# VectorE's order within a score step: bank evacuations ahead of page sums, pool differences, normalisation products and sample sums

## The reference

```
h = rms_norm(x);  z = h @ w_in            # one projection, 3624 columns
q, k, v, ga, qi, wi, ki, ub, gb, uc, gc = split(z)
att  = softmax attention of 8 heads over the 132 (sample: 64) keys that relu indexer scores choose
pool = (trailing mean over 2/4/8/16 tokens - token) @ pool_w * pool_scale      # from ub
conv = silu(layer_norm(causal depthwise conv of width 31 (cv * sigmoid(cg))))
x    = x + concat(att * silu(ga), pool * silu(gb), conv * silu(gc)) @ w_out
```

## Time and profile before

| | us |
|---|---|
| median of 3 runs | 739.81 |
| lowest and highest run | 735.61, 743.48 |
| the profiled execution, its own time | 738.43 |
| its span from the first to the last instruction | 737.1 |

### The profile page before, as it was taken

The page is one execution under the profiler, slowest core; times in us unless marked ns, Lnnn a source line. Parts: engine busy times, 40 slices in busy tenths (PEclk is TensorE's granted clock), DMA queues, the critical chain, the costliest instruction groups (busy, mean ns, idle before and its releaser), DMA issues.

```text
span 737.1 us, 14658 instructions
## 1 busy us (share of the span) xinstructions
PE 688.2 (93%) x5314; PEld 576.1 (78%) x5314; DVE 521.5 (71%) x1312; ACT 342.5 (46%) x884; POOL 311.1 (42%) x463
## 2 busy tenths in 40 slices
PE   5999989799889989999999998978989898999998
PEld 5987868588787777768999686757878787777797
DVE  4358989899977876445733998999997795722232
ACT  5747536245946433333245762734484643332202
POOL 1403599963947600111250259997384861000000
PEclk9999999899989999999999999999998998999999
DMA  5460240314223525015016213131423164401302
GB/s 206 141 196 19 69 135 30 116 36 145 59 89 112 201 70 199 0 58 174 22 59 190 58 60 101 75 116 36 145 59 89 58 174 145 172 1 58 103 20 109
DMA packets 54984, 71.97 MB, mean 98 GB/s; under 512 B 12977, under 2 KB 30585, under 8 KB 54881
## 3 DMA queue, kind: packets, MB, share of 16 engines
q1 hardware_dynamic: 54802, 70.96, 30.0%
q10 hardware_dynamic: 111, 0.08, 0.0%
HBM read 64.05 MB, written 7.61 MB: 97 GB/s over the span
## 4 chain that ended last, share of the span: by engine, by line
PE 43%; DVE 21%; POOL 14%; ACT 10%; DMA 5%; issue 4%; SPq 2%; DVEq 0%; POOLq 0%; ACTq 0%
PE R L1347 16%; DVE bias L1791 5%; DVE small L1789 4%; PE R L1331 4%; PE R L1332 3%; PE R L1333 3%; POOL small L907 3%; ACT W_r L986 3%; ACT W L986 3%; PE R L1490 3%; DVE W_r L1695 3%; POOL kz L911 3%; PE A L1519 2%; PE A L1277 2%; POOL kz L909 2%
## 5 line engine op out<-in xcount | busy, mean ns | idle before, releaser
L1331 PE MATMUL R<-x_hi,W_r 128*128 128x268 f32 x448 | 138.6, 309 | 5.9 <-DVE cc L1695 1.8
L865 POOL TENSOR_TENSOR W_r<-W,W_r 128x256 fp32r<-128x256 f32 x128 | 92.1, 751 | 114.7 <-ACT W_r L986 114.0
L1333 PE MATMUL R<-x_hi,W_r 128*128 128x268 f32 x448 | 132.4, 295 | 0.0
L1332 PE MATMUL R<-x_lo,W_r 128*128 128x268 f32 x448 | 132.2, 295 | 0.0
L1347 PE MATMUL R<-yT,W 128*128 128x268 f32 (+2 forms) x768 | 124.2, 318 | 0.0
L1347 PEld LDWEIGHTS R<-yT,W 128*128 128x128 f32 x768 | 106.9, 190 | 15.8 <-issue 7.1
L1306 PE MATMUL R<-W_r,x_hi 128*128 128x512 f32 (+2 forms) x252 | 98.8, 392 | 15.1 <-DVE W_r L1695 11.5
L1331 PEld LDWEIGHTS R<-x_hi,W_r 128*128 128x128 f32 x448 | 88.6, 198 | 22.0 <-issue 10.6
L1307 PE MATMUL R<-W_r,x_hi 128*128 128x512 f32 (+2 forms) x252 | 95.6, 379 | 0.0
L1308 PE MATMUL R<-W_r,x_lo 128*128 128x512 f32 (+2 forms) x252 | 95.2, 378 | 0.0
L1332 PEld LDWEIGHTS R<-x_lo,W_r 128*128 128x128 f32 x448 | 88.9, 198 | 0.0
(11 more groups left out here) (277 smaller groups left out, 1300.4 us busy)
## 6 DMA issues: line engine op xcount, KB each, us to landing
W<-in_w_in SPq DMA_DIRECT2D x52, 512.0 KB, 4.8
KV<-in_cache_k SPq DMA_DIRECT2D x32, 256.0 KB, 2.9
W<-in_w_out SPq DMA_DIRECT2D x8, 1024.0 KB, 7.5
KV<-in_cache_v SPq DMA_DIRECT2D x32, 256.0 KB, 3.4
ubx<-qkv_rows SPq DMA_DIRECT2D x16, 256.0 KB, 3.4
out_new_k_prompt<-kz SPq DMA_DIRECT2D x8, 256.0 KB, 2.0
out_new_v_prompt<-V SPq DMA_DIRECT2D x8, 256.0 KB
out_y_prompt<-W SPq DMA_DIRECT2D x8, 256.0 KB
```

The costliest lines, as they stand in the source:

```text
L865: done = pool.tensor_tensor(w_raw(m, W_r)[part], w_raw(m)[part], w_high(m, W_r)[part].bitcast(F32), ALU.subtract)
L1331: pe.matmul(out, hi[:, cols], x_hi[:, kc, toks], start=(kc == 0), stop=False)
L1332: pe.matmul(out, hi[:, cols], x_lo[:, kc, toks], start=False, stop=False)
L1333: m = pe.matmul(out, lo[:, cols], x_hi[:, kc, toks], start=False, stop=(kc == KC - 1))
```

## The change

Within DVE's score step `take` moves from the end of the step to the place behind the sample tokens' top-k, logits and value work and ahead of the normalisation product `on`; and `pool_differences`, `ln_diag`, `ln_mul`, `swish`, `page_scores`, and the sample tokens' sums (of step 26 those behind "isc", and all of step 27) move behind `on`. The first two instructions of step 26 (the reduction and scaling "isc"), step 6's sample dots, the sample tokens' top-k and softmax, and the product `y_s` at the very end of a step stay in their order to `take`. No instruction is added, removed or altered, and the other four engines' programs are the same.

```diff
                 late(n)
-                if n == SX["pool_diff"]:
-                    pool_differences(0)
-                if n == SX["pool_diff2"]:
-                    pool_differences(1)
-                if n == SX["ln_diag"]:
...
-                if n == SX["ln_mul"]:
...
-                if 0 <= n - SX["swish"] < 3:
...
-                b = n - SX["pages"]
-                if 0 <= b < 8:
-                    page_scores(2 * b)
-                    page_scores(2 * b + 1)
                 if n == SX["index_dots"]:
...
                 if n == SX["index"]:
                     sd(lambda: dve.reduce_sum(isc.rearrange("p (g b) -> p g b", g=2), ds[:, :, :, :], AX.X))
                     sd(lambda: dve.tensor_scalar(isc, isc, 1.0 / 16, None, ALU.mult), "isc")
-
-                    dve.wait_ge(*rows_s.at(32))
...
-                if n == SX["index_turn"]:
...
+                if n < len(PLAN):
+                    for u in PLAN[n]:
+                        if u[0] not in ON_ACT:
+                            take(u)
                 if n >= 11 and (n - 11) % 8 == 0:
                     i = (n - 11) // 8
                     dve.wait_ge(*MV_s.at(i + 1))
                     wait_evac(dve, ("turn", i, 0))
                     tile = qT[:, :, START[i]:START[i] + ROWS[i]]
                     on_s.did(dve.tensor_tensor(tile, A[:, 2, :].rearrange("p (c t) -> p c t", c=4)[:, :, 0:ROWS[i]], tile, ALU.mult))
-                if n < len(PLAN):
-                    for u in PLAN[n]:
-                        if u[0] not in ON_ACT:
-                            take(u)
+                if n == SX["index"]:
+                    dve.wait_ge(*rows_s.at(32))
...
+                if n == SX["index_turn"]:
...
+                if n == SX["pool_diff"]:
+                    pool_differences(0)
+                if n == SX["pool_diff2"]:
+                    pool_differences(1)
+                if n == SX["ln_diag"]:
+                    dve.wait_ge(*lnp_s.at(2))
+                    dve.wait_ge(*pd_s.at(PD_END))
+                    for i in range(NT):
+                        r = LN_ROWS[i]
+                        lnd_s.did(dve.tensor_scalar(ln_dg[0:r, 128 * i:128 * i + r], ident[0:r, 0:r], lnr[0:r, i:i + 1], None, ALU.mult))
+                if n == SX["ln_mul"]:
...
+                if 0 <= n - SX["swish"] < 3:
...
+                b = n - SX["pages"]
+                if 0 <= b < 8:
+                    page_scores(2 * b)
+                    page_scores(2 * b + 1)
                 for at, tile, lo, hi in ((29, 2, 0, HALF), (38, 3, HALF, START[4]), (43, 4, START[4], NTOK)):
```

More of the change, by code:

```diff
@@ L2042, in vector_layer @@
                 late(n)
-                if n == SX["pool_diff"]:
-                    pool_differences(0)
-                if n == SX["pool_diff2"]:
-                    pool_differences(1)
-                if n == SX["ln_diag"]:
[L2048 to L2052, removed]
-                if n == SX["ln_mul"]:
-                    wait_evac(dve, ("lnrow", 0, 1))
-                    ln_s.did(dve.tensor_tensor(cc[:, :, :], cc[:, :, :], lnrow.unsqueeze(1).broadcast_to([128, 2, TOK]), ALU.mult))
-                if 0 <= n - SX["swish"] < 3:
-                    if n == SX["swish"]:
-                        dve.wait_ge(*gate_s.at(GATE_OF["gc", 1, 1] + 1))
-                    swish(n - SX["swish"])
-                b = n - SX["pages"]
-                if 0 <= b < 8:
-                    page_scores(2 * b)
-                    page_scores(2 * b + 1)
                 if n == SX["index_dots"]:
@@ L2124, in vector_layer @@
                     on_s.did(dve.tensor_tensor(tile, A[:, 2, :].rearrange("p (c t) -> p c t", c=4)[:, :, 0:ROWS[i]], tile, ALU.mult))
-                if n < len(PLAN):
-                    for u in PLAN[n]:
-                        if u[0] not in ON_ACT:
-                            take(u)
+                if n == SX["index"]:
+                    dve.wait_ge(*rows_s.at(32))
+                    sd(lambda: dve.tensor_tensor(t8[:, :, 0:ID], zis[:, 0:256].rearrange("p (h d) -> p h d", h=IH),
+                                                 zis[:, 256:288].unsqueeze(1).broadcast_to([8, IH, ID]), ALU.mult))
+                    sd(lambda: dve.reduce_sum(d8, t8[:, :, 0:ID], AX.X))
+                    sd(lambda: stt(e8, d8, 0.0, zis[:, 384:392], ALU.max))
+                    sd(lambda: dve.reduce_sum(sc8[:, 256:257], e8, AX.X))
+                    sd(lambda: dve.tensor_scalar(sc8[:, 256:257], sc8[:, 256:257], 1.0 / 16, None, ALU.mult))
@@ new lines, in vector_layer @@
+                if n == SX["index_turn"]:
+                    sd(lambda: dve.tensor_tensor(t8, rows8[:, 0:512].rearrange("p (h d) -> p h d", h=8),
+                                                 rows8[:, 512:1024].rearrange("p (h d) -> p h d", h=8), ALU.mult))
+                    sd(lambda: dve.reduce_sum(snw, t8, AX.X))
+                    sd(lambda: dve.tensor_tensor(sn.rearrange("p (b h) -> p b h", b=8), E8.rearrange("p (b h) -> p b h", b=8),
+                                                 snw.unsqueeze(1).broadcast_to([8, 8, 8]), ALU.mult))
+                    dve.wait_ge(*sit_s.at(1))
+                    sd(lambda: dve.tensor_copy(sc8[:, 0:256], A[0:8, 3, 0:256]))
@@ new lines, in vector_layer @@
+                if n == SX["ln_mul"]:
+                    wait_evac(dve, ("lnrow", 0, 1))
+                    ln_s.did(dve.tensor_tensor(cc[:, :, :], cc[:, :, :], lnrow.unsqueeze(1).broadcast_to([128, 2, TOK]), ALU.mult))
+                if 0 <= n - SX["swish"] < 3:
+                    if n == SX["swish"]:
+                        dve.wait_ge(*gate_s.at(GATE_OF["gc", 1, 1] + 1))
+                    swish(n - SX["swish"])
+                b = n - SX["pages"]
+                if 0 <= b < 8:
+                    page_scores(2 * b)
+                    page_scores(2 * b + 1)
```

## The result

The changed kernel takes **743.28 us** (median; 738.68 to 749.19) against 738.45 for the kernel before on the same chip: ratio **1.0063** (95%: 1.0041 to 1.0084). It is 0.63% slower, which is 4.65 us of 738.45. The forecast was 738.0, 1.8 us faster than the 739.81 that it started from. The time lies in the forecast's range, and a change within 1% was its likeliest case, but the sign is wrong. Ratios leave out disturbed executions, so they need not equal the quotient of two medians.

A forecast was written before the change was run, and what follows sets the result against it. The prediction took PE, busy 93% of the span, as the bound, so only its idle time could move. +0.4 and -2.2 us summed to -1.8, from 739.81 to 738.0 us, range 733.5 to 744.5.

The forecast's parts named there:

- Step 12: Pool differences and diagonals end 1.6 and 2.2 us later; PE's stop before lnrow0 grows to about 3.5 and 3.4 us.
- Step 16: At `weigh`, ACT's earlier copy gives part of the delay back; PE released +0.5 and +0.3 to +0.8 us late.
- the swap of slow units: Second layer: gc01 turns slow at the low clock, +1.3 us, and gc10 turns fast, -1.3 us.
- the prediction's own sign: The prediction counts as wrong if PE leaves step 16 more than 1 us late.
- the second layer's -2.2 us of steps 26 to 28: ga31 starts 3.2 or 1.5 us earlier, depending on ga30's clock; -2.2 us taken.
- the last page sum: Page sums of steps 18 to 25: the last comes +0.8 us in the first layer, -0.4 in the second.
- +0.4 for steps 26 to 28 of the first layer: PE's ga31 starts 0.4 us later, as ga21's evacuation comes 1.5 us later.
- The move of the sums: Step 26: 1.33 us of sample sums move behind the evacuation; turn2 starts 0.5 and 1.7 us earlier.
- step 28: First layer: 2.75 us of moved work precedes its mask, gate and top-k; ga21's evacuation 1.5 us later.
- The diagonals' rival: Step 12's delay not given back, plus slow gc01: 5.1 us together, 744.8 us; chance of slower 0.18.
- The first rival: More gain: last page sum not late in first layer, clock holds through second layer's ga30; about -5, 734.8 us; chance 0.14.
- Nothing moves: PE's time stays and every stop only changes its name: 739.8 us; chance 0.13.

The follow-up runs named there:

- before_third: The kernel before, unaltered, run and profiled once more as its third profile: 737.25 us.
- diag_only: Kernel before with only the pool differences and diagonals of DVE's score step 12 moved behind gc00's evacuation: 741.89 us, ratio 1.0063.
- layer0_change: Kernel before with the new order in the first layer's score loop only, the old order in the second: 741.17 us, ratio 1.0011.
- sums_only: Kernel before with only the sample tokens' sums of steps 26 and 27 moved behind the evacuations, `on` staying ahead: 733.87 us, ratio 0.9939.
- on_swish_only: Kernel before with only `on` and `swish` moved behind the evacuations, the page sums staying ahead, so also ahead of `swish`: 747.93 us, ratio 1.0124.
- sums_diff10: Kernel before with the sample sums behind the evacuations and the second pool differences issued in step 10 instead of 12: 748.33 us, ratio 1.0133.
- diag_ahead: Changed kernel with the pool differences and diagonals of step 12 put back ahead of gc00's evacuation: 740.00 us, ratio 1.0032.

## Why the forecast was wrong

**Step 12** was right: 3.58 and 3.59 us before lnrow0, forecast 3.5 and 3.4. **Step 16** was right in kind: the stop at `weigh` is gone, and `weigh` came 0.42 and 0.45 us later in two of three profiles of the first layer (forecast +0.5); in the third gc01 ran at 0.65, not at 0.93 and 0.84, and it was +1.59. In the second layer the swap of slow units came as forecast, gc10's -1.0 in the mean against +1.34 ahead of it, a net of +0.3. One of the three profiles of the kernel before (before_third) has gc01 slow and gc10 fast too, so the swap is not the change's alone. diag_only, which has only this part, is 0.63% or 4.7 us slower, though (0.25 to 1.02%): the part is not as cheap as these stages make it. By the prediction's own sign (PE leaves step 16 more than 1 us late) this step told against it in four of the six stages.

**The step that failed is the second layer's -2.2 us of steps 26 to 28**: the stage from ga11 to ga31 came out at +1.1 in the mean (-0.50 and +1.56). Two readings in it were wrong. First, the 2.1 us that ga30 lost to the clock were taken as part of the old order's time, which an earlier start would partly save. They were chance, not a fixed part of it: in the other two profiles of the kernel before this ga30 runs at full clock. The row is before_third's busy time by stretch, ga30 of the second layer:

```profile
618.50:621.70 3.20, 3.20 (x28) 3.20 (x26) 2.73 (x6) 0.60 (x1) 0.00 (x0) 1.00 0.00 0
```

In the changed kernel it is slow in all three profiles (0.73, 0.61, 0.72). The old order is not free of it: in layer0_change, whose second layer has that order, ga30 ran at 0.64. But a loss that comes and goes cannot be counted as saved. Second, the last page sum was put at -0.4 us there. The loads of pages 14 and 15 leave SP here (before, then after, both layers):

```profile
251.58 0.89 SPq L674 DMA_DIRECT2D KV<-in_cache_k  x2
...
605.74 0.89 SPq L674 DMA_DIRECT2D KV<-in_cache_k  x2
```

```profile
255.23 0.89 SPq L674 DMA_DIRECT2D KV<-in_cache_k  x2
...
612.67 0.89 SPq L674 DMA_DIRECT2D KV<-in_cache_k  x2
```

ga11 started at 248.30 and 603.24 before, 251.27 and 608.71 after, so they left 3.28 and 2.50 us behind it, and 3.96 in both layers now. The means of three profiles are 3.00 and 2.64 before, 3.88 and 3.70 after: **+0.9 (forecast +0.8) and +1.1 (forecast -0.4)**. The last page sum itself ended 11.11, 11.07 and 10.53 us behind the start of the second layer's ga11 before, and 12.13, 11.53 and 12.08 after: +1.0.

The wait that decides is the one for `swish`. DVE's last `swish` products and SP's first DMA behind its wait, first layer (before, then after):

```profile
248.43 1.88 DVE L1695 SCALAR_TENSOR_TENSOR yT<-qkT,yT 128x536 f32<-128x536 f32 x2
...
250.34 0.32 SPq L805 DMA_DIRECT2D qkT<-qkv_rows  x1
```

```profile
251.88 2.08 DVE L1695 SCALAR_TENSOR_TENSOR yT<-qkT,yT 128x536 f32<-128x536 f32 x2
...
253.99 0.32 SPq L805 DMA_DIRECT2D qkT<-qkv_rows  x1
```

In all three profiles of both kernels SP goes on some 0.03 us behind the end of `swish`, and the loads leave 1.25 to 1.27 us behind it. `swish` ended 1.73 and 1.39 us behind the start of ga11 before (first and second layer, means) and 2.61 and 2.45 after, so its +0.9 and +1.1 are the whole delay of the loads. The forecast named this wait, but let earlier evacuations outweigh it in the second layer. Which of the pieces that now stand ahead of `swish` holds it back was not separated.

A third error is in the sum itself: step 16's +0.5 and +0.3 to +0.8 were not in it, as if PE's delay would vanish in the later wait for the page sums. It does not, because the page sums stand between evacuations and move with PE: in diag_only the loads leave 3.4 us behind ga11's start in the first layer, no sooner than before, and turn2 comes 14.66 us behind it.

These terms close the loops' balance: +0.4 for steps 26 to 28 of the first layer, as forecast, +0.8 and +0.3 for step 16 and the slow units, +1.1 for steps 26 to 28 of the second layer, together the +2.6.

**The move of the sums** was right: in sums_only turn2 comes 1.2 and 1.6 us earlier (forecast 1.33 for the sums alone), and in the changed kernel step 28 gives 0.87 us back (turn2 to ga31 with ga30 at full clock: 11.03 and 11.04 us, against 10.17). The gain is there and is spent by other parts of the same change: `swish` and page sums behind the evacuations (putting both back is worth 0.86%) and the diagonals (0.63% alone; 0.3% in the changed kernel, not clear of noise). The parts do not add up (0.63 - 0.61 + 0.32 + 1.24 = 1.58% against 0.63%); two reasons fit, that the late `swish` and the late page sums hold back the same two loads, and that `swish` stands further back in on_swish_only than in the changed kernel, but neither was itself tried.

**The rivals.** The diagonals' rival gave 744.8 and is nearest to 743.3, and its point of decision (more than 0.8 us late at `weigh`) was passed in four of the six stages of the table. But step 16 gave more back than it said: by the stages step 12 and the slow units cost +0.8 and +0.3 us net, not 5.1 together, and with the diagonals put back half of the loss stays (1.0032). That it came near is in part luck. The first rival asked for the last page sum on time and a clock that holds through ga30; sums_only, another kernel, has both, to 0.3 us, and comes near its 734.8. "Nothing moves" fell.

**What stays open.** The loops account for 2.6 of the 4.65 us. From the start of the span to the first ub30 unchanged code took 199.8, 199.5 and 199.3 us before and 202.3, 200.5 and 198.0 after; such differences are as large as what is missing, so the rest can't be placed. The granted clock, on record for every timed execution, points at a part of it: it is 0.974 in the mean of 117 executions of the kernel before and 0.970 in 31 of the changed one, and within either kernel an execution with 0.010 less took some 3.3 us longer. By that slope 0.004 goes with 1.3 us (an estimate); which stretches they lie in is not shown.

## What to carry to other kernels

"Evacuations first" is no rule for a whole step: each piece that it pushes back has its own reader, and the gain came from the one piece (the sample sums) that held back an evacuation and that PE does not wait for soon. Follow the reader through every queue: `swish` reached PE by way of SP's loads, POOL's product and DVE's own later step. And before a stretch at the low clock enters a sum, look for it in a second profile of the same kernel.

## What the runs showed of the hardware

A DVE product of two SBUF inputs that started with POOL's run of eight products was held for the whole of it: 5.57 us in place of 0.19, and 5.70 in the second layer (sums_diff10). The gate of ub30, whose two inputs also lie in SBUF, ran into a run of POOL in both kernels: 2.62 us before (205.97) and 2.63 after (208.49), against 0.44 for later gates. An evacuation, with one input in PSUM, took its usual 0.44 us in the middle of such a run in sums_only (203.13, POOL's run from 201.33 to 206.87). The Trainium skill, "GPSIMD Engine Reference", section "8. Key points", names this contention for DVE instructions with two SBUF inputs; the trace agrees. Beside POOL's page products the loss was smaller: a `swish` product took 0.70 us with POOL idle (before, 249.60) and 1.25 us beside them (after, 252.72).

The clock fell behind each stop of 3.6 us: lnrow0's eight matmuls ran at a granted clock of 0.50, 0.60 and 0.50 in the first layer and 0.84, 0.50 and 0.87 in the second, in the three profiles of the changed kernel, and took 2.04, 1.75, 2.05 and 1.26, 2.05, 1.22 us, against 1.13 at 1.00 in the earlier trace rows. At turn2 the length of the stop did not decide: ga30 ran at 1.00 behind 2.40 us (before_third, second layer) and behind 2.51 (diag_ahead, second layer), and at 0.73 behind 2.17 (after, second layer). What does decide was not found.
